# Reordered dilation-4 attention blocks, earlier key staging, and regrouped work in the output projection

## The chip, the cores and the metric

The kernel runs on one core of one Trainium2 chip. The core has five engines with an instruction queue each: TensorE (PE, matmuls; its weight loads are shown as PEld), VectorE (DVE), ScalarE (ACT), GpSimd (POOL) and SyncE (SP), which here does nothing but issue DMAs. The engines run side by side and wait for one another by semaphores. The metric is the device time of one execution in microseconds (us). The kernel before takes 2401.49 us, the median of three runs between 2398.72 and 2403.63. A difference of 0.2% is 4.8 us.

## The reference

One decoder layer over 2048 tokens of width 1024, in float32: a mixer with three head groups (gated linear attention, a gated recurrence, and dilated sliding-window attention), an output projection with a residual, then a gated convolutional FFN. The change touches the dilated attention and the output projection. The attention has six heads of 64 and three patterns:

```python
DILATED_PATTERNS = ((128, 1), (512, 4), (2048, 16))   # (window, dilation)
for window, dil in DILATED_PATTERNS:
    L = S // dil                                      # each residue class mod dil is a sequence of its own
    o, lse = banded_causal_attention(to_sub(q), to_sub(k), to_sub(v), window // dil)
w = softmax(stack(lses), axis=0)                      # the patterns are weighed by their log-sum-exps
o_c = rms_norm(einsum('pbsh,pbshd->bshd', w, stack(outs)), swa_norm)
x = x + concatenate([o_a, o_b, o_c]) @ w_out
```

In banded_causal_attention a block of 128 queries sees its own 128 keys and the 128 before them. The first block of a sequence has no block before it and sees 128 keys only.

## The kernel before

The program runs four parts one after the other: mixer_front, dilated_attention, output_projection and conv_ffn. Between mixer_front and dilated_attention, and between dilated_attention and the output projection, all engines meet at a barrier.

**dilated_attention** goes through 40 turns, one block of queries of all six heads each (attention_blocks, L1180). A turn is j, its block (pattern, residue r, block b). Turns 0 to 15 are dilation 1. Turns 16 to 23 are dilation 16, "double" turns: two residue classes of 128 tokens at once, each with 128 keys. Turns 24 to 39 are dilation 4: before, b is the outer loop, so turns 24 to 27 are the four first blocks (128 keys, `first(j)`), and turns 28 to 39 are full blocks (256 keys).

The engines work on a turn in a pipeline. In iteration j PE does the scores of turn j in three pairs of heads (L1802), and between them it turns the probabilities of turn j-1 (L1814), multiplies them with the values (sums, L1834) and, from turn 24 on, turns the normalised outputs of turn j-3 (L1847). DVE takes the maxima (L1650, L1653, L1658), copies half of the turned probabilities (L1666), finds the lower of two maxima (find_low, L1676), takes the sums (take_sums, L1694), and normalises (L1713, L1717) and stores outputs (take_outputs, L1704). ACT does the exponentials (L1563), the other turned probabilities (L1571) and the weights (L1595). POOL weighs and joins the turn with what an earlier pattern left (L1514, L1519).

The order on each engine is the order of the program text. Points that the change touches:
- **Staging.** For dilation 16 and 4 the keys and queries are gathered with a stride into k_s and q_s, two buffers used by j % 2. POOL copies the keys in `stage(j)` (L1482): two copies for a double turn (L1492), one for a first block (L1494), and three for a full block, its queries included (L1496 to L1498). For double turns and first blocks ACT copies the queries (stage_queries, L1582). PE's scores(j, 0) waits for `staged` and `q_staged`.
- **Weight sums.** Ahead of its first stage POOL does 11 times sum_weights (L1521), four additions on a slab of a later matrix that SP loads and stores again. stage(16) comes after the last of them.
- **Values.** Values in token order lie in v_tok, a ring of 8 slots. SP writes those of dilation 1 to memory (store_values, L1385), and loads them back with a stride (load_values, L1389). Before, a turn of dilation 4 has the slot j % 8. The rows of the earlier pattern are loaded by load_rows (L1401), which waits for `joined` of the turn three before it.
- **Outputs.** The outputs of four turns fill out[:, b % 2]. SP stores them in store_out (L1438) at turns 32 and 36, after load_rows of that SP turn. take_outputs of the first turn of b = 2 (turn 32) waits until store_out(0) has landed, since it overwrites its buffer.

**output_projection** multiplies 32 products n = 8 b + m (b: 512 tokens, m: 128 output columns), each of 8 steps of three matmuls. ACT begins with a table load (L2110). DVE splits the weight slabs (weights_low, L2166), then drains product n into the residual (L2241); PE's product n waits for drain n - 4. After the first product of b = 1, 2, 3 PE sums the squares of block b - 1 (L2262), for which POOL adds them up (L2149) and which ACT turns into a root (L2106).

Of the kernel before, what the change touches and what calls it, by code (L numbers as in the profile page):

```python
# [10 lines left out]
ALU = mybir.AluOpType  # L11
# [5 lines left out]
KT = D // P  # L17
S = 2048
# [1150 lines left out]
SPAN = 128  # L1169
# [13 lines left out]
def attention_blocks():  # L1183


    for b in range(TILES_0):
        yield 0, 0, b
    for r in range(DILATIONS[1]):
        for b in range(2):
            yield 2, r, b  # L1190
    for b in range(S // (DILATIONS[1] * SPAN)):
        for r in range(DILATIONS[1]):
            yield 1, r, b


def dilated_attention(nc, proj_t, ident, swa_gain, v_scratch, o_scratch, mix_t, w_down, s_t,
# [3 lines left out]
    with ExitStack() as ctx:  # L1200
# [112 lines left out]
        def v_slot(j):  # L1313

            return 2 * (j - TILES_0) % V_RING if double(j) else j % V_RING

        def v_half(j, half):

            pat, r, b = blocks[j]
            if pat == 2:  # L1320
                return v_slot(j) + half
            if b == 0:
                return v_slot(j) if half == 0 else (v_slot(j) + V_RING - 1 if pat == 0 else v_slot(j) + 4) % V_RING
            return v_slot(j) if half else (j - (1 if pat == 0 else 4)) % V_RING

        def v_known(engine, j):

            if j < TILES_0:
                engine.wait_ge(v_ready, j + 1)
            elif double(j):  # L1330
                engine.wait_ge(v_in[v_slot(j)], 16 * ((j - TILES_0) // 4 + 1))
            else:
                engine.wait_ge(v_in[v_slot(j)], 16 * ((j - FIRST_1) // V_RING + 1 + (2 if v_slot(j) % 2 == 0 else 0)))
# [39 lines left out]
        def _(sp):  # L1373
# [64 lines left out]
            def store_out(b):  # L1438
                sp.wait_ge(out_ready, 4 * (b + 1))
                sp.dma_start(mix_t[5:8, :, blk(b)].rearrange("g p s -> p g s"), out[:, b % 2, :, :]).then_inc(out_stored[b % 2], 16)  # L1440
# [9 lines left out]
            for j in range(TURNS):  # L1450
# [21 lines left out]
                if j >= FIRST_1 + 8 and (j - FIRST_1) % 4 == 0:  # L1472
                    store_out((j - FIRST_1) // 4 - 2)
# [8 lines left out]
        def _(pool):  # L1482
# [52 lines left out]
            for i in range(KP):  # L1535
                sum_weights(i)
            for j in range(TILES_0 - 1, TURNS + 4):
# [15 lines left out]
        def _(act):  # L1553
# [57 lines left out]
            for j in range(TURNS + 5):  # L1611
# [14 lines left out]
                if TILES_0 <= j + 2 < FIRST_1 + DILATIONS[1]:  # L1626
                    stage_queries(j + 2)
# [11 lines left out]
        def _(dve):  # L1639
# [56 lines left out]
            def take_outputs(i):  # L1696
                f = i - FIRST_1
                b, r = f // 4, f % 4
# [61 lines left out]
        def _(pe):  # L1760
# [10 lines left out]
            def scores(j, g):  # L1771
                pat, r, b = blocks[j]
                if g == 0:
# [5 lines left out]
                    else:  # L1779
                        pe.wait_ge(staged, staged_after(j))  # L1780
                        if double(j) or first(j):
                            pe.wait_ge(q_staged, j - TILES_0 + 1)
# [141 lines left out]
def output_projection(nc, block, used, mix_t, x_t, w_slabs, norm_gain, rstd, x2_t, h_t, origin, w_loaded, mix_loaded, out_stored,  # L1924
# [3 lines left out]
    with ExitStack() as ctx:  # L1928
# [139 lines left out]
        def _(act):  # L2068
# [41 lines left out]
            act.preload_act_table_set("natural_log_exp_and_others")  # L2110
# [46 lines left out]
        def _(dve):  # L2157
# [28 lines left out]
            for n in range(2, OUT_SLABS):  # L2186
                weights_low(n)
# [46 lines left out]

            for b in range(BLOCKS):
                dve.wait_ge(x_loaded[b % 2], 16 * (b // 2 + 1))
                for m in range(KT):
                    n = KT * b + m
                    dve.wait_ge(product_done, n + 1)
                    at = xs[b][:, m, :]  # L2240
                    dve.tensor_tensor(at, banks[n % 4][:, :], at, ALU.add).then_inc(added, 1)  # L2241
# [13 lines left out]
        def _(pe):  # L2255
# [20 lines left out]
            for b in range(BLOCKS):  # L2276
                for m in range(KT):
# [7 lines left out]
                    if n == KT:  # L2285
                        pe.wait_ge(w_ready, 1)
                    cols = slice(m * P, (m + 1) * P)
                    product(pe, banks[n % 4][:, :],
                            [w_hi[:, k, cols] for k in range(KT)], [w_lo[:, k, cols] for k in range(KT)],
                            [mix_hi[b % 2][:, k, :] for k in range(KT)],  # L2290
                            [mix_lo[b % 2][:, k, :] for k in range(KT)], range(KT),
                            mix_ready if b and m == 0 else None, KT * b).then_inc(product_done, 1)
                    if b and m == 0:
                        sum_squares(b - 1)
# [1022 lines left out]
```

## Time and profile before

| | |
|---|---|
| runs | 2398.72, 2401.49, 2403.63 us |
| the profiled execution | 2398.96 us, its span 2397.2 us |
| PE busy, share of the span | 98% |
| DVE, ACT, POOL busy | 72%, 47%, 37% |
| attention turns 16 to 39 | 738.65 to 916.6 us of the span |
| output projection | 919.56 to 1098.9 us |

The busy time of PE counts pipelined matmuls with modelled ends, so it says that PE is hardly ever without work, not that it works at its peak. PEclk is the clock that TensorE was granted, 1.00 for 2.4 GHz and 0.50 for 1.2 GHz. A time in brackets behind a row is how long the engine stood idle before it, and what ended that.

### The profile page before, as it was taken

What the parts mean: (1) busy time and instruction counts of PE and PEld (TensorE: products, weight loads), DVE (VectorE), ACT (ScalarE), POOL (GpSimd) and SP (SyncE); (2) the same over time, 40 slices, a digit from 0 to 9 for tenths busy, and PEclk for the clock granted to TensorE, in tenths of its full rate; (3) what the DMA queues carried; (4) which work ended last, traced back from release to release, by engine and by line L of the source; (5) the groups of instructions that cost most, each with busy time, mean ns of one, the idle gap of its engine ahead of it and who ended that gap; (6) DMA issues with size and microseconds to landing.
All of it is one profiled execution on the core that took longest, in us unless ns stands there. A gap on an engine that the chain in (4) does not pass through costs nothing.

```text
span 2397.2 us, 32989 instructions
## 1 busy us (share of the span) xinstructions
PE 2337.3 (98%) x11664; PEld 1896.7 (79%) x11664; DVE 1719.1 (72%) x2527; ACT 1133.6 (47%) x2026; POOL 888.8 (37%) x705
## 2 busy tenths in 40 slices
PE   8999999999999998999999999999999999999997
PEld 6777888878777776887788888788788888887886
DVE  6454558995455675357888888769979888887655
ACT  6634354332346665225544444545654444445443
POOL 0000003441066672224565656230446565652211
PEclk9999999999999898999999999999999999999999
DMA  5333325553796337374232223598533232337764
GB/s 176 114 98 110 101 83 172 173 178 121 251 313 225 106 105 252 115 254 177 104 125 108 112 102 115 185 307 258 163 125 117 110 110 102 115 117 265 224 197 141
DMA packets 191795, 379.04 MB, mean 158 GB/s; under 512 B 17168, under 2 KB 62864, under 8 KB 182416
## 3 DMA queue, kind: packets, MB, share of 16 engines
q1 hardware_dynamic: 191632, 376.94, 46.3%
q8 instruction: 93, 1.52, 0.3%
q14 instruction: 70, 0.57, 0.1%
HBM read 252.90 MB, written 123.98 MB: 157 GB/s over the span
## 4 chain that ended last, share of the span: by engine, by line
PE 55%; DVE 4%; issue 1%; ACT 1%; DMA 0%; DVEq 0%; ACTq 0%; SPq 0%
PE ff_bank L81 16%; PE ff_bank L82 16%; PE ff_bank L83 16%; PE op_bank L75 2%; PE op_bank L74 2%; PE op_bank L73 2%; DVE ff_ring L3006 1%; DVE ff_b_lo L2948 1%; DVE ff_x_first L3027 0%; DVE ff_y_gate L2993 0%; DVE ff_ring L2954 0%; DVE ff_y_val L2993 0%; PE op_bank L81 0%; DMA ff_raw<-in_slabs 0%; ACT ff_ring L2742 0%
## 5 line engine op out<-in xcount | busy, mean ns | idle before, releaser
L82 PE MATMUL ff_bank<-ff_b_lo,ff_ring 128*128 128x512 f32 x1232 | 479.9, 390 | 0.0
L81 PE MATMUL ff_bank<-ff_b_hi,ff_ring 128*128 128x512 f32 x1056 | 413.2, 391 | 9.5 <-ACT ff_e L2752 5.1
L83 PE MATMUL ff_bank<-ff_b_hi,ff_ring 128*128 128x512 f32 x1056 | 411.7, 390 | 0.0
L73 PE MATMUL ip_bank<-ip_x_hi,ip_w_hi 128*128 128x512 f32 x704 | 289.8, 412 | 12.3 <-DVE ip_x_lo L722 10.6
L74 PE MATMUL ip_bank<-ip_x_lo,ip_w_hi 128*128 128x512 f32 x704 | 276.3, 392 | 0.0
L75 PE MATMUL ip_bank<-ip_x_hi,ip_w_lo 128*128 128x512 f32 x704 | 276.0, 392 | 0.0
L82 PEld LDWEIGHTS ff_bank<-ff_b_lo,ff_ring 128*128 128x128 f32 x1232 | 231.8, 188 | 48.4 <-issue 0.5
L81 PE MATMUL ff_bank<-ff_ring,ff_ring 128*128 128x512 f32 x616 | 241.4, 392 | 2.9 <-DVE ff_ring L3006 2.9
L81 PEld LDWEIGHTS ff_bank<-ff_b_hi,ff_ring 128*128 128x128 f32 x1056 | 198.7, 188 | 54.4 <-issue 7.4
L82 PE MATMUL ff_bank<-ff_ring,ff_ring 128*128 128x512 f32 x616 | 239.7, 389 | 0.0
L83 PE MATMUL ff_bank<-ff_ring,ff_ring 128*128 128x512 f32 x616 | 239.7, 389 | 0.0
L83 PEld LDWEIGHTS ff_bank<-ff_b_hi,ff_ring 128*128 128x128 f32 x1056 | 198.6, 188 | 41.3
L2954 DVE TENSOR_TENSOR ff_ring<-ff_raw,ff_ring 128x512 fp32r<-128x512 f32 x219 | 216.6, 996 | 13.0 <-ACT ff_ring L2742 12.0
L3006 DVE TENSOR_TENSOR ff_ring<-ff_raw_ring,ff_ring 128x512 fp32r<-128x512 f32 x196 | 142.9, 773 | 57.6 <-ACT ff_ring L2790 57.4
L2993 DVE SCALAR_TENSOR_TENSOR ff_y_gate<-ff_u,ff_conv_all,ff_y_gate 128x1024 f32<-128x1024 f32 x88 | 164.1, 1865 | 13.9 <-ACT ff_y_gate L2775 11.3
L73 PEld LDWEIGHTS ip_bank<-ip_x_hi,ip_w_hi 128*128 128x128 f32 x704 | 133.1, 189 | 43.9 <-issue 11.1
L2790 ACT ACTIVATE ff_ring<-ff_raw_ring 128x512 fp32r<-128x512 f32 x196 | 112.3, 623 | 110.6 <-PE ff_bank L83 99.1
L2752 ACT ACTIVATE ff_e<-ff_bank 128x512 f32<-128x512 f32 x132 | 78.5, 595 | 168.3 <-PE ff_bank L83 161.4
L751 DVE TENSOR_TENSOR ip_staged<-ip_bank,ip_rstd 128x512 f32<-128x512 f32 x76 | 52.0, 688 | 144.9 <-PE ip_bank L75 139.3
L75 PEld LDWEIGHTS ip_bank<-ip_x_hi,ip_w_lo 128*128 128x128 f32 x704 | 133.0, 189 | 28.9
L74 PEld LDWEIGHTS ip_bank<-ip_x_lo,ip_w_hi 128*128 128x128 f32 x704 | 133.3, 189 | 27.5 <-issue 2.6
L2993 DVE SCALAR_TENSOR_TENSOR ff_y_val<-ff_u,ff_conv_all,ff_y_val 128x1024 f32<-128x1024 f32 x88 | 114.0, 1296 | 56.6 <-ACT ff_y_val L2775 54.9
(333 smaller groups left out, 4896.4 us busy)
## 6 DMA issues: line engine op xcount, KB each, us to landing
ff_raw<-in_slabs SPq DMA_DIRECT2D x44, 1024.0 KB, 4.9
proj_t<-ip_staged SPq DMA_DIRECT2D x92, 256.0 KB, 2.7
a_t<-ff_y_val SPq DMA_DIRECT2D x44, 512.0 KB, 2.6
t_t<-ff_t_sum SPq DMA_DIRECT2D x88, 256.0 KB, 2.0
ff_raw_ring<-t_t SPq DMA_DIRECT2D x56, 256.0 KB, 4.1
ff_raw_ring<-s_t SPq DMA_DIRECT2D x52, 256.0 KB, 3.3
rp_tables<-in_rope SPq DMA_DIRECT2D x24, 512.0 KB, 4.4
ff_raw_ring<-in_w_down SPq DMA_DIRECT2D x46, 256.0 KB, 3.6
```

The source lines that it names most:

```text
L73: pe.matmul(out, w_hi[k], x_hi[k], start=(k == 0), stop=False)
L74: pe.matmul(out, w_hi[k], x_lo[k], start=False, stop=False)
L75: last = pe.matmul(out, w_lo[k], x_hi[k], start=False, stop=(k == n - 1))
L81: pe.matmul(out, w_hi, x_hi, start=first, stop=False, skip_group_check=resumed)
L82: pe.matmul(out, w_hi, x_lo, start=False, stop=False, skip_group_check=resumed)
L83: return pe.matmul(out, w_lo, x_hi, start=False, stop=last, skip_group_check=resumed)
L751: dve.tensor_tensor(at, bank, scale, ALU.mult).then_inc(bank_free, 1)
L2752: act.activation(e[:, i, :], banks[X[g % 2]][:, :], ACT.Copy).then_inc(e_ready[i], 1)
L2790: act.activation(ring[to][:, 0, :], raw_at(half, n, i), ACT.Copy).then_inc(d_hi_ready, 1)
L2954: dve.tensor_tensor(ring[at][:, 1, :], source(half, m), ring[at][:, 0, :].bitcast(F32), ALU.subtract).then_inc(w_lo_ready, 1)
L2993: dve.scalar_tensor_tensor(out=at, in0=u[:, a, t:t + HALF], scalar=conv_all[:, g, a, t:t + 1], in1=at, op0=ALU.mult, op1=ALU.add).then_inc ...
L3006: dve.tensor_tensor(ring[to][:, 1, :], raw_at(half, n, i), ring[to][:, 0, :].bitcast(F32), ALU.subtract).then_inc(d_lo_ready, 1)
```

## The change

Four things are done.

1. attention_blocks yields the first two blocks of each residue class of dilation 4 together, r0 b0, r0 b1, r1 b0, r1 b1 and so on (turns 24 to 31); turns 32 to 39 stay as they were. The slots of the values follow from r and b, ACT stages the queries of all first blocks, PE's count of `q_staged` is adapted, and store_out(0) and store_out(1) move to SP turns 35 and 36.
2. POOL does stage(16) before the last sum_weights, not after it.
3. The table load at the head of ACT's part of the output projection is gone, and DVE drains products 0 and 1 before it splits the last weight slab.
4. PE's sum of squares stands in the middle of the second product of a block, not behind the first.

```diff
     for r in range(DILATIONS[1]):
         for b in range(2):
             yield 2, r, b
-    for b in range(S // (DILATIONS[1] * SPAN)):
+    for r in range(DILATIONS[1]):
+        for b in range(2):
+            yield 1, r, b
+    for b in range(2, S // (DILATIONS[1] * SPAN)):
         for r in range(DILATIONS[1]):
             yield 1, r, b
...
         def v_slot(j):
 
-            return 2 * (j - TILES_0) % V_RING if double(j) else j % V_RING
+            pat, r, b = blocks[j]
+            return 2 * (j - TILES_0) % V_RING if double(j) else j % V_RING if pat == 0 else r + 4 * (b % 2)
...
-                engine.wait_ge(v_in[v_slot(j)], 16 * ((j - FIRST_1) // V_RING + 1 + (2 if v_slot(j) % 2 == 0 else 0)))
+                engine.wait_ge(v_in[v_slot(j)], 16 * (blocks[j][2] // 2 + 1 + (2 if v_slot(j) % 2 == 0 else 0)))
...
             def store_out(b):
-                sp.wait_ge(out_ready, 4 * (b + 1))
+                sp.wait_ge(out_ready, 7 if b == 0 else 4 * (b + 1))
...
-                if j >= FIRST_1 + 8 and (j - FIRST_1) % 4 == 0:
-                    store_out((j - FIRST_1) // 4 - 2)
+                if j in (FIRST_1 + 11, FIRST_1 + 12):
+                    store_out(j - FIRST_1 - 11)
...
-            for i in range(KP):
+            for i in range(KP - 1):
                 sum_weights(i)
-            for j in range(TILES_0 - 1, TURNS + 4):
+            stage(TILES_0)
+            sum_weights(KP - 1)
+            for j in range(TILES_0, TURNS + 4):
...
-                if TILES_0 <= j + 2 < FIRST_1 + DILATIONS[1]:
+                if j + 2 < TURNS and (double(j + 2) or FIRST_1 <= j + 2 and first(j + 2)):
                     stage_queries(j + 2)
...
-            act.preload_act_table_set("natural_log_exp_and_others")
             for k in range(4):
                 act.sem_inc(mix_hi_ready, 1)
...
-            for n in range(2, OUT_SLABS):
-                weights_low(n)
+            weights_low(2)
...
+            drain(0)
+            drain(1)
+            weights_low(3)
             for b in range(BLOCKS):
...
-                    if b and m == 0:
-                        sum_squares(b - 1)
+                    for ks in (range(KT // 2), range(KT // 2, KT)):
+                        ins = product(pe, banks[n % 4][:, :], ..., ks, ...)
+                        if b and m == 1 and ks[0] == 0:
+                            sum_squares(b - 1)
+                    ins.then_inc(product_done, 1)
```

`drain(n)` is the wait, the addition and the increment that stood in the loop of L2241 before.

## Rows read from the trace of the kernel before

**Rows 1.** The page: busy time of the engines, and the chain that ended last.
```profile
PE 2337.3 (98%) x11664; PEld 1896.7 (79%) x11664; DVE 1719.1 (72%) x2527; ACT 1133.6 (47%) x2026; POOL 888.8 (37%) x705
...
PE 55%; DVE 4%; issue 1%; ACT 1%; DMA 0%; DVEq 0%; ACTq 0%; SPq 0%
```

**Rows 2.** What PE waited for, 690 to 925 us: total, times, longest.
```profile
PE at_s L1791 <- POOL at_k_s L1492: 4.5, 1, 4.5
```

**Rows 3.** Windows cut at PE's scores(j, 0): length, busy by engine, PEclk, DMA.
```profile
738.65:748.12 9.47, 9.47 (x69) 7.59 (x69) 3.57 (x6) 4.07 (x14) 3.07 (x4) 0.74 0.59 200
748.12:755.10 6.98, 6.98 (x68) 5.96 (x67) 4.07 (x8) 5.31 (x16) 0.76 (x3) 1.00 0.56 187
...
802.85:807.00 4.15, 3.91 (x31) 2.91 (x30) 3.43 (x16) 2.41 (x8) 3.93 (x3) 1.00 0.30 108
807.00:811.95 4.95, 4.17 (x32) 3.00 (x31) 3.73 (x18) 3.10 (x10) 3.12 (x6) 0.99 0.53 163
811.95:818.97 7.02, 7.02 (x34) 5.57 (x33) 4.10 (x18) 5.37 (x20) 6.04 (x10) 0.50 0.38 115
818.97:827.28 8.31, 8.31 (x34) 5.58 (x34) 5.24 (x19) 4.35 (x12) 4.22 (x7) 0.50 0.17 49
827.28:836.28 9.00, 9.00 (x52) 6.73 (x52) 5.61 (x19) 4.22 (x11) 4.24 (x7) 0.72 0.16 47
836.28:843.00 6.72, 6.72 (x52) 5.24 (x51) 5.35 (x19) 4.70 (x14) 5.01 (x7) 1.00 0.21 60
```

**Rows 4.** The same columns: a long wait of PE in the FFN.
```profile
1115.00:1130.00 15.00, 10.66 (x39) 8.06 (x38) 14.49 (x16) 7.27 (x14) 7.22 (x5) 0.89 0.15 51
```

**Rows 5.** POOL's timeline: start, length, instruction, idle before.
```profile
731.78 1.27 POOL L1526 TENSOR_TENSOR at_w_sums<-at_w_sums 128x512 f32<-128x512 f32 x1 [2.37 <-DMA at_w_sums<-in_w_down]
...
737.02 3.10 POOL L1492 COPY at_k_s<-at_qkv 128x384 f32<-128x384 f32 x4
```

**Rows 6.** SP's DMA issues, and the DVE instruction that waits for the rows.
```profile
742.01 0.37 SPq L1399 DMA_DIRECT2D at_v_tok<-v_scratch  x1
...
748.72 0.32 SPq L1383 DMA_DIRECT2D o_scratch<-at_o_sb  x1
750.71 0.37 SPq L1412 DMA_DIRECT2D at_rows<-o_scratch  x1
...
754.09 0.17 DVE L1676 TENSOR_TENSOR at_o_sb<-at_neg,at_rows 128x12 f32<-128x12 f32 x1 [0.33 <-DMA at_rows<-o_scratch]
```

**Rows 7.** DMA landing, us: value loads of turns 16, 17; output stores.
```profile
at_v_tok<-v_scratch SPq DMA_DIRECT2D x1, 390.0 KB, 3.6
...
at_v_tok<-v_scratch SPq DMA_DIRECT2D x1, 390.0 KB, 4.2
...
DMA to landing us min/median/max: 3.6/4.5/6.6
```

**Rows 8.** Staging of turn 25, sums of turn 23; copies by form.
```profile
800.38 0.87 POOL L1494 COPY at_k_s<-at_qkv 128x384 f32<-128x384 f32 x1
...
802.95 0.97 DVE L1694 TENSOR_TENSOR at_o_sb<-at_o,at_weight 128x780 f32<-128x780 f32 x1 [1.16 <-PE at_o L1834]
...
L1497 POOL COPY at_k_s<-at_qkv 128x384 f32<-128x384 f32 x12 | 13.9, 1162 | 0.0
...
L1666 DVE COPY at_probs_t<-at_t 128x256 f32<-128x256 f32 x8 | 3.4, 420 | 0.9 <-PE at_t L1814 0.8
```

**Rows 9.** Iteration 36: SP's load of rows, DVE's take_outputs(32), PE's turn_outputs(33).
```profile
878.97 0.32 SPq L1412 DMA_DIRECT2D at_rows<-o_scratch  x1
...
881.03 0.84 DVE L1704 TENSOR_TENSOR at_out<-at_o,at_gain 128x384 f32<-128x384 f32 x1
...
882.02 0.52 PE L1847 MATMUL at_o<-gl_idf,at_o_f 128*128 128x128 f32 x3
```

**Rows 10.** Output projection: ACT's table load, DVE's drain of product 0.
```profile
919.22 1.28 ACT L2110 ACT_TABLE_LOAD   x1 [3.59 <-PEq L64]
...
942.31 0.69 DVE L2241 TENSOR_TENSOR op_x_first<-op_bank,op_x_first 128x512 f32<-128x512 f32 x1
```

More of the change, by code:

```diff
@@ L1323, in v_half @@
                 return v_slot(j) if half == 0 else (v_slot(j) + V_RING - 1 if pat == 0 else v_slot(j) + 4) % V_RING
-            return v_slot(j) if half else (j - (1 if pat == 0 else 4)) % V_RING
+            return v_slot(j) if half else (j - 1) % V_RING if pat == 0 else r + 4 * ((b - 1) % 2)
         def v_known(engine, j):
@@ L1697, in take_outputs @@
                 f = i - FIRST_1
-                b, r = f // 4, f % 4
+                _, r, b = blocks[i]
                 dve.wait_ge(turned_out, f + 1)
@@ L1781, in scores @@
                         if double(j) or first(j):
-                            pe.wait_ge(q_staged, j - TILES_0 + 1)
+                            pe.wait_ge(q_staged, j - TILES_0 + 1 if double(j) else DOUBLE + r + 1)
                 if GROUPS * j + g >= GROUPS * FIRST_1 + 2:
@@ L2185, in _, with drain @@
                 low(0, k)
-            for n in range(2, OUT_SLABS):
-                weights_low(n)
+            weights_low(2)
+            def drain(n):
+                b, m = n // KT, n % KT
+                if m == 0:
+                    dve.wait_ge(x_loaded[b % 2], 16 * (b // 2 + 1))
+                dve.wait_ge(product_done, n + 1)
+                at = xs[b][:, m, :]
+                dve.tensor_tensor(at, banks[n % 4][:, :], at, ALU.add).then_inc(added, 1)
             def norm(b, k):
@@ L2233, in lows_at @@
                 return range(m + 1 if m else 0, min(m + 2, KT))
+            drain(0)
+            drain(1)
+            weights_low(3)
             for b in range(BLOCKS):
-                dve.wait_ge(x_loaded[b % 2], 16 * (b // 2 + 1))
                 for m in range(KT):
[L2238 to L2241, printed above, removed]
+                    if KT * b + m >= 2:
+                        drain(KT * b + m)
                     if b + 1 < BLOCKS:
@@ L2287, in _ @@
                     cols = slice(m * P, (m + 1) * P)
[L2288 to L2292, printed above, removed]
-                    if b and m == 0:
-                        sum_squares(b - 1)
+                    for ks in (range(KT // 2), range(KT // 2, KT)):
+                        ins = product(pe, banks[n % 4][:, :],
+                                      [w_hi[:, k, cols] for k in range(KT)], [w_lo[:, k, cols] for k in range(KT)],
+                                      [mix_hi[b % 2][:, k, :] for k in range(KT)],
+                                      [mix_lo[b % 2][:, k, :] for k in range(KT)], ks,
+                                      mix_ready if b and m == 0 else None, KT * b)
+                        if b and m == 1 and ks[0] == 0:
+                            sum_squares(b - 1)
+                    ins.then_inc(product_done, 1)
         return product_done, added, first_low_ready, slab_summed, summed, square_ready
```

## The prediction

> **What bounds the kernel now.** I read the page first: PE is busy 98% of the span and leads the chain that ended last [rows 1]. So time can come only from PE's waits, or from its clock. Next come PE's waits around the attention. The longest that work inside the attention causes is one of 4.5 us for POOL's staged keys [rows 2]. Third come windows cut at scores(j, 0) [rows 3]. They show what a list of waits can't: two stretches in which PE works at 1.2 GHz. The first holds iteration 16 (9.47 us at a mean clock of 0.74, while iteration 17 with the same work takes 6.98). The second goes from 811.3 to about 832 us and holds iterations 27, 28 and most of 29 (clock 0.50, 0.50, 0.72). Before it PE had waited 4.15 - 3.91 = 0.24 and 4.95 - 4.17 = 0.78 us in the turns with 128 keys. The full turns of dilation 4 behind it run at 1.00 and 6.72 us each.
>
> **Step A, the first staging.** POOL ends sum_weights(9) at 729.4 and then stands idle 2.37 us until the slab of the last one lands at 731.78; the staging starts only at 737.02 [rows 5]. A pair of copies costs 3.10 / 2 = 1.55 us, so stage(16) now runs from 729.4 to 731.0, inside that idle time, and the last sum_weights keeps its times. stage(17) ends at 738.6, before PE asks for it at 741. PE goes from turn 15 into scores(16, 0) at 734.1 without a wait and at full clock: iteration 17 would start at 734.1 + 6.98 = 741.1, not at 748.12. That is 7.0 us: 4.5 of the wait and 2.5 of the clock.
>
> What is late next hangs on SP's queue, which doesn't move. store_values(15) stands in it behind the store of the last weight sums, so the values of turn 16 are loaded only at 742.01 [rows 6], and land 3.6 us later, at 745.6 [rows 7]. PE wants them in sums(16, 0), some 2.6 us into iteration 17, at 743.7: a new wait of 1.9 us. Then the rows: store_sums(15) stood at 748.72 and landed 2.0 us later, and load_rows(16) followed at 750.71. Now the store goes out at about 743.4, right behind the value load of turn 17, which goes out 0.9 us after that of turn 16 and lands 4.2 us later, at 747.1 [rows 7]; so I let the store land at 747.6, an estimate. The rows come 3.3 us after their issue, as from 750.71 to 754.0, at 751.0. DVE's find_low(16), at 754.09 before, wants them at 753.8 - 7.0 + 1.9 = 748.7 and waits 2.3 us. Behind it queue take_sums(16), the maxima of turn 18 and the copy for sums(17, 0), which has some 0.5 us to spare. PE loses 1.7 more. A is worth 7.0 - 1.9 - 1.7 = 3.4 us. Bounds: 7.0 if both loads come early enough, 1 if low clock comes back for a few us.
>
> **Step B, the alternation.** PE's work is the same set of blocks. At full clock, without waits, iterations 25 to 29 would cost 3.91, 3.91, 4.26 (with turn_outputs: 0.52 long, 0.35 until the next [rows 9]), 4.91 (full scores: 8.31 - 7.02 = 1.29 more at 1.2 GHz, so 0.65 at 2.4) and 6.72, together 23.7 us. They took 836.28 - 802.85 = 33.4 [rows 3]. So 9.7 us lie there: 1.0 of waits, 8.7 of clock. The clock part goes if it stays up; the waits change.
>
> - Turn 25 is now a full block. stage(25) is three copies, two like the 0.87 at 800.38 and one of 1.16 [rows 8], some 2.8 us in place of 0.87, and ends at 803.2. PE wanted it at 802.85 (0.35 late). log_weights(23) and ACT's weights(23) queue behind it, so take_sums(23) starts at 803.85, not 802.95. Behind the 0.9 of take_sums come the maxima of two heads at 256 keys, 0.7 (an estimate), and the copy, 0.4: ready at 805.85. PE, with two scores and two turns of probabilities before it, 2.0 us, wants it at 805.25 (0.6 late).
> - Iteration 26 has about 0.2 of the same kind.
> - Later pairs: PE has 4.91 + 6.07 = 10.98 us for a pair (full scores with first sums, and the other way round). DVE is busy 5.35 in a full turn [rows 3]. In the half with full scores only its two copies shrink, to 0.42 each [rows 8], which leaves 4.8 against PE's 4.9; in the other half its maxima shrink, which leaves some 4.5 against 6.1. So PE waits some 0.4 a pair (between 0 and 1), three times. POOL, 5.01 in a full turn and 1.9 less in one that stages a first block, needs 8.1 of 11; ACT is busy 4.70 in a full turn.
>
> Sum of the new waits 0.35 + 0.6 + 0.2 + 1.2 = 2.35 (1 to 4). B is worth 9.7 - 2.35 = 7.35 us at full clock.
>
> **Step C, the store of outputs.** store_out(0) moves from SP turn 32 to 35, behind load_rows(37). That load waits for the join of turn 34 and went out at 878.97, in iteration 36. So the store is issued at 879.3 and lands 3.6 to 6.6 us later, median 4.5 [rows 7], at 883.8. take_outputs(32) overwrites that buffer and stood at 881.03 [rows 9]. It now waits 2.8 us and ends at 884.7. PE's turn_outputs(33) needs it and stood at 882.02. PE loses 2.7 us (1.8 to 4.8); DVE's maxima(36, 2) and take_sums(35) queue behind, but reach the next iteration in time. store_out(1) keeps its place. This step costs 2.7 us that the kernel before doesn't have.
>
> **Steps at nothing.** The table load, 1.28 us at 919.22 [rows 10]: PE's first twelve matmuls run 5 us from 919.56 on at the low clock, and what ACT feeds first, the fifth k, needs a conversion on ACT and one on DVE of 0.7 us each behind the load, so it is ready by 922. No load stood at the head of ACT's attention part either, so none is put in its place. The drains: drain 0 ends at 943.0 [rows 10] and PE's product 4 follows without a wait; it now ends earlier. The slab that moves behind it is for products 6 and 7, two products later. The sum of squares comes half a product, 2.7 us, later; two of its roots stand on ACT behind loads that come later still, and the third is followed by a long idle stretch of ACT. If that cover went, each could cost the 1 or 2 us by which it is late; a gain needs a wait of PE there, and PE has none between 925 and 1098.
>
> The Trainium skill, page "ScalarE: Activation LUTs", section "What ACT_TABLE_LOAD costs", gives about 1283 ns for the load and a drain of about 1380 ns more. The trace has the 1283 but no drain: ACT goes on at 920.51. By either figure the sum stays, as it is ACT's time and not PE's.
>
> **The sum.** -3.4 - 7.35 + 2.7 = -8.0 us. On the profiled execution, 2398.96 us (span 2397.2 and 1.8 around it), that is 2391. The median of the runs is 2401.49, 2.5 above that execution; I take the change from the median: **2393 us**.
>
> **Rivals.**
> 1. *The low clock moves into the alternation and lasts.* For it: before 811.3 PE had waited 0.24 and 0.78 us in two turns, and I forecast 0.35, 0.6 and 0.2 within 8. Once low, the clock stayed low through a turn with full scores and first sums (8.31 us at 0.50), although PE didn't wait, and rose only in a turn of full blocks. The alternation has no such iteration before 32. If it falls in 26 or 27 and stays till 32, 27 us of work cost 8.31 / 4.91 = 1.69 times as much, +18.6, in place of 8.7 before, and the short waits cancel. Total -3.4 + 18.6 - 8.7 + 2.7 = +9: 2411. It is slower than before from an excess of 3.4 + 8.7 - 2.7 = 9.4 us on, about 23 us of low clock (8.7 came of 21). Against it: full blocks carry more work per turn, and in the FFN PE idled 4.3 of 15 us and the clock was at 0.89, 3.3 us of low clock, no more [rows 4].
> 2. *It falls there but comes back as it did.* The excess is 4 to 9 us in place of 8.7, the waits about even; total -5 to 0: 2396 to 2401.
> 3. *The clock falls for some 5 us at A or C*, where PE stands still 1.9 and 2.7 us: +2 to +4 on the forecast, 2396.
> 4. *No new waits at A or C*, because the loads and the store land at their fastest or the order leaves them room: another 3 to 5 us off, 2389.
>
> The Trainium skill's page "TensorE: Matmul & The Clock Gate", section "A second HAM failure mode: psum-queue depth-cycling", says that frequent short idles between groups of matmuls are enough to make the clock swing. The fall at 811.3 after waits of under a us a turn agrees. By that rule the new short waits could bring it down as well, which is rivals 1 and 2; by the rows of full blocks alone it would stay up.
>
> **Chances.** Forecast 0.44 (own range 2389 to 2396), rival 1 0.10, rival 2 0.15, rival 3 0.18, rival 4 0.13. A run of this kernel can tell 0.2%, 4.8 us, from no change. Faster: nearly all of the forecast and of rival 4, and 0.07 of rivals 2 and 3: 0.63. Within 0.2%: 0.26. Slower: rival 1 and an edge of 2: 0.11. The range that leaves out rival 1 and the best of 4 is 2386 to 2404.
>
> **What would show it.** After: no idle before scores(16, 0) and clock 1.00 in iteration 16; a wait of about 2 us at sums(16, 0) and an idle of 2 us for DMA before L1676 of turn 16; clock 1.00 in iterations 25 to 31, 5 to 6 us each; in iteration 36 an idle of 2.8 us on DVE before L1704, ended by the store of outputs, and 2.7 on PE. Wrong would be a clock of 0.5 anywhere between 800 and 840, no wait in iteration 36, or any change of the output projection's length of 179 us beyond 1 us.

## The result and the profile after

The changed kernel takes 2405.1 us (median of 20 runs), the kernel before 2398.5 (median of 20 beside them). The ratio is 1.0028, 95% interval 1.0019 to 1.0037: slower by some 6.7 us, where I had forecast 8.0 faster. (My 2393 stood on the median of three runs of the kernel before, 2401.49, which is 3.0 above that of the twenty; so I compare changes.) The profiled execution spans 2407.8 us, 10.6 more than the one before.

The first view is again the windows cut at PE's scores(j, 0): length, busy time by engine, PEclk, DMA. Iterations 15 to 20 of the changed kernel (they answer to the first two of [rows 3]):

```profile
728.88:736.43 7.55, 7.49 (x59) 5.60 (x58) 4.73 (x8) 4.80 (x10) 6.70 (x7) 1.00 0.99 369
736.43:743.61 7.18, 7.18 (x68) 5.99 (x67) 4.62 (x8) 5.14 (x15) 5.64 (x6) 1.00 0.46 183
743.61:751.92 8.31, 7.21 (x67) 5.98 (x66) 3.89 (x7) 5.14 (x14) 0.00 (x0) 1.00 0.55 149
751.92:764.28 12.36, 9.68 (x67) 8.08 (x66) 4.71 (x9) 7.04 (x17) 8.27 (x11) 0.78 0.70 227
764.28:773.46 9.18, 9.18 (x67) 7.70 (x66) 4.19 (x7) 4.07 (x15) 3.34 (x6) 0.73 0.57 179
773.46:780.43 6.97, 6.97 (x67) 5.96 (x66) 4.32 (x7) 5.44 (x16) 5.25 (x7) 1.00 0.22 55
```

The reader is to see that iterations 15 and 16 are clean, and that iterations 17 to 19 then give it back: a wait of 1.1 us in 17, one of 2.7 in 18, and a low clock behind it. The six iterations take 51.55 us. Before they took 776.01 - 726.62 = 49.39.

Iterations 25 to 32, the alternation (the other rows of [rows 3]):

```profile
807.35:812.51 5.16, 4.55 (x30) 2.92 (x30) 3.95 (x16) 3.09 (x8) 4.43 (x5) 1.00 0.23 80
812.51:818.98 6.47, 5.92 (x50) 4.92 (x49) 4.76 (x18) 3.56 (x12) 5.36 (x9) 1.00 0.57 186
818.98:823.94 4.96, 4.75 (x35) 3.19 (x34) 4.22 (x18) 4.86 (x14) 3.04 (x5) 1.00 0.27 81
823.94:830.67 6.73, 6.38 (x53) 5.27 (x52) 5.08 (x19) 4.77 (x16) 5.20 (x8) 1.00 0.21 63
830.67:835.99 5.32, 4.87 (x35) 3.28 (x34) 4.79 (x19) 4.35 (x12) 2.72 (x5) 1.00 0.26 76
835.99:842.86 6.87, 6.38 (x53) 5.27 (x52) 5.05 (x19) 4.99 (x17) 5.32 (x9) 1.00 0.19 59
842.86:848.80 5.94, 4.86 (x34) 3.27 (x33) 5.42 (x19) 3.67 (x11) 4.68 (x7) 1.00 0.23 72
848.80:855.93 7.13, 6.98 (x52) 5.27 (x52) 5.33 (x19) 5.16 (x15) 5.14 (x8) 1.00 0.19 58
```

The clock stays at 1.00. Length less busy time gives a short wait in every iteration. The eight take 48.58 us, 53.60 before: 5.0 gained.

Iterations 36 to 38, around the store of outputs:

```profile
876.08:885.52 9.44, 6.86 (x53) 5.31 (x52) 5.41 (x19) 4.82 (x15) 5.02 (x7) 0.98 0.37 127
885.52:897.66 12.14, 12.14 (x52) 9.41 (x51) 5.69 (x19) 6.64 (x19) 5.49 (x8) 0.50 0.29 98
897.66:906.48 8.82, 8.82 (x53) 6.54 (x52) 5.61 (x19) 3.10 (x7) 3.80 (x6) 0.74 0.59 173
```

They take 30.40 us, 20.16 before: 10.2 lost, of which 2.6 is a wait. Iteration 37 has no wait at all and takes 12.14 us, because PE runs at 1.2 GHz from end to end. The timelines of SP, DVE and PE show what the wait hangs on (start, length, instruction, idle time before it and what ended it; they answer to [rows 9]):

```profile
878.46 0.32 SPq L1416 DMA_DIRECT2D at_rows<-o_scratch  x1
878.83 0.43 SPq L1444 DMA_DIRECT2D mix_t<-at_out  x1
...
883.14 0.83 DVE L1710 TENSOR_TENSOR at_out<-at_o,at_gain 128x384 f32<-128x384 f32 x1 [2.54 <-DMA mix_t<-at_out]
...
884.12 0.52 PE L1853 MATMUL at_o<-gl_idf,at_o_f 128*128 128x128 f32 x3 [2.58 <-DVE at_out L1710]
```

The same for turn 16 (they answer to [rows 6]): the values of turn 16 go out at 743.66, the store of turn 15's sums at 746.05, and only when that has landed do the rows go out, at 750.88. For PE's wait of 1.10 us at the values the profile names no releaser ("issue"); that it is the load of the values is my reading of the order, and loads_and_store_early below bears it out: with that load earlier the wait is gone.

```profile
743.66 0.37 SPq L1403 DMA_DIRECT2D at_v_tok<-v_scratch  x1
...
746.05 0.42 SPq L1387 DMA_DIRECT2D o_scratch<-at_o_sb  x1
...
747.46 1.08 PE L1840 MATMUL at_o<-at_v_tok,at_probs_t 128*128 128x65 f32 x8 [1.10 <-issue]
...
750.88 0.37 SPq L1416 DMA_DIRECT2D at_rows<-o_scratch  x1
...
754.15 0.17 DVE L1682 TENSOR_TENSOR at_o_sb<-at_neg,at_rows 128x12 f32<-128x12 f32 x1 [3.56 <-DMA at_rows<-o_scratch]
...
757.35 1.11 PE L1840 MATMUL at_o<-at_v_tok,at_probs_t 128*128 128x65 f32 x8 [2.68 <-DVE at_probs_t L1672]
```

The rest of the 10.6 us: turn 15 starts 2.3 us later, the part behind the output projection is 1.6 longer, and the unchanged iterations, the attention's tail and the projection together 0.6 shorter. The projection takes 1108.36 - 928.91 = 179.45 us up to PE's first matmul of the FFN, where it took 1099.36 - 919.56 = 179.80. Nothing that was changed runs in the first of these or the second; over all fourteen profiles below the start of turn 15 lies anywhere between 722.91 and 730.52 us.

### The profile page after: what moved, and what is told of

Same layout as the page of the kernel before. It is cut to its first block, busy times and chain, and to the rows that moved or that the text cites. A ratio compares the mean times of both kernels' runs of the same rounds, so it can differ in the third digit from the quotient of the medians.

```text
span 2407.8 us, 32989 instructions
## 1 busy us (share of the span) xinstructions
PE 2342.9 (97%) x11664; PEld 1900.0 (79%) x11664; DVE 1717.9 (71%) x2527; ACT 1133.4 (47%) x2025; POOL 886.8 (37%) x705
## 4 chain that ended last, share of the span: by engine, by line
PE 55%; DVE 4%; issue 1%; ACT 1%; DMA 0%; DVEq 0%; ACTq 0%; SPq 0%
PE ff_bank L81 16%; PE ff_bank L82 16%; PE ff_bank L83 16%; PE op_bank L74 2%; PE op_bank L75 2%; PE op_bank L73 2%; DVE ff_ring L3021 1%; DVE ff_b_lo L2963 1%; DVE ff_x_first L3042 0%; DVE ff_ring L2969 0%; DVE ff_y_val L3008 0%; DMA ff_raw<-in_slabs 0%; DVE ff_y_gate L3008 0%; PE op_bank L81 0%; DVE ff_x_second L3036 0%
```

## The experiments

Each ran 12 times beside the kernel before, the three repeats of a profile once. All profiles are cut at the same three stretches, and the table after the last experiment has them side by side.

### The store of outputs: store_early and late_store_alone

```diff
-                if j in (FIRST_1 + 11, FIRST_1 + 12):
-                    store_out(j - FIRST_1 - 11)
+                if j in (FIRST_1 + 10, FIRST_1 + 12):
+                    store_out((j - FIRST_1 - 10) // 2)
```

> The changed kernel with store_out(0) one turn of SP's queue earlier: behind load_rows(36) instead of load_rows(37). Nothing else is changed. Theory (step C, with a low clock behind the wait): the store lands near 877, take_outputs(32) finds it done, PE's wait of 2.6 us in iteration 36 goes, and with it the low clock of iterations 37 and 38: iterations 36 to 38 take 20.2 us in place of 30.4, all at clock 1.00, and the time is 10 us under the changed kernel's, about 2395. Rival 1 (the low clock in iterations 37 and 38 has another cause, the short waits of the alternation before it): only the wait goes, 2.6 us, iterations 37 and 38 stay at 12 and 8.8 us, 2402.5. Rival 2 (the store only moves the wait to another turn, since take_outputs waits for other stores too): no gain, 2405.

Measured: 2395.3 us, ratio 0.9989 (0.9975 to 1.0003), 9.8 us under the changed kernel. Iterations 36 to 38 take 6.72, 6.72 and 6.71 us at clock 1.00. One line, one turn of the queue, gives back more than the whole loss of 6.7 us. The theory holds and both rivals fall. Against the kernel before, the 2.9 us that are left can't be told from nothing.

late_store_alone is the reverse, on the kernel before:

```diff
-                if j >= FIRST_1 + 8 and (j - FIRST_1) % 4 == 0:
-                    store_out((j - FIRST_1) // 4 - 2)
+                if j in (FIRST_1 + 11, FIRST_1 + 12):
+                    store_out(j - FIRST_1 - 11)
```

> The kernel before, in its old order of blocks, with nothing changed but store_out(0) put behind load_rows(37) (SP turn 35). Theory: the same wait of 2.6 us in iteration 36 arises, the clock falls behind it, and iterations 36 to 38 take about 30 us in place of 20.2: 10 us slower than the kernel before, ratio 1.004. Rival 1 (my step C): only the wait, 2.7 us, ratio 1.001. Rival 2 (the low clock needs the alternation's short waits ahead of it): the wait, but clock 1.00 behind it, again 2.7 us.

Measured: 2404.7 us, ratio 1.0026 (1.0014 to 1.0039), 6.5 slower than the kernel before. So the late store needs no alternation ahead of it to cost two to three times what its wait is long. The windows of its iterations 36 and 37:

```profile
877.98:888.42 10.44, 7.86 (x52) 6.31 (x51) 5.42 (x19) 5.76 (x19) 5.83 (x8) 0.83 0.34 116
888.42:896.64 8.22, 8.22 (x52) 5.95 (x51) 5.60 (x19) 3.87 (x9) 3.83 (x7) 0.80 0.41 145
```

The wait is 2.58 us as in the changed kernel, but the low clock behind it is shorter (25.4 us for the three iterations in place of 30.4). I had expected about 30, so the size of what the clock adds was not yet understood.

### The early staging: stage_as_before and staging_alone

```diff
-            for i in range(KP - 1):
+            for i in range(KP):
                 sum_weights(i)
-            stage(TILES_0)
-            sum_weights(KP - 1)
-            for j in range(TILES_0, TURNS + 4):
+            for j in range(TILES_0 - 1, TURNS + 4):
```

> The changed kernel with the first staging put back behind the last sum of weights. Theory (step A is worth nothing once the clock falls in iteration 18): PE waits 4.5 us for POOL again before scores(16, 0), the wait of 1.1 us at sums(16, 0) and the one of 2.7 us behind find_low(16) go, the clock falls in iteration 16 only (0.74), and turn 15 to turn 21 take 49.4 us in place of 51.6: the time is 2 us less than the changed kernel's, 2403. Rival (step A is worth the 3.4 us of my prediction and the changed kernel's low clock there is an accident of one execution): 3.4 us more than the changed kernel, 2408.5.

Measured: 2402.6 us, ratio 1.0025 (1.0012 to 1.0038), 2.5 under the changed kernel. That seems to say that step A is a loss. But the intervals overlap, and its profile has turns 15 to 20 at 49.15 us and iterations 36 to 38 at 25.7, not 30.4: most of the difference lay in a stretch that this edit doesn't touch. So step A had to be priced where no late store stands behind it. staging_alone is the same edit the other way round, on the kernel before:

> The kernel before with the early first staging and nothing else. It prices step A where no late store and no alternation stand behind it. Theory (from the profiles so far: turn 15 to turn 21 took 46.8, 46.8 and 51.6 us with the early staging and no other load order, 49.2 to 51.8 with the late one): 1 to 3 us under the kernel before, ratio 0.9990; so step A is a small gain and the 2.5 us by which stage_as_before was under the changed kernel come from the clock behind the late store, 25.7 us there against 30.4 and 31.2. Rival 1: step A is a loss by itself, +2.5 us, ratio 1.001. Rival 2: my step A, -3.4 us, ratio 0.9986.

Measured: 2399.1 us, ratio 1.0000 (0.9987 to 1.0013). By itself step A is worth nothing that can be measured; the interval is 3.1 us to either side, so my 3.4 is out and a loss of 2.5 isn't settled. Its windows show why, iterations 17 and 18:

```profile
739.48:747.88 8.40, 7.21 (x67) 5.98 (x66) 3.89 (x7) 5.14 (x14) 0.00 (x0) 1.00 0.61 180
747.88:759.84 11.96, 10.48 (x68) 8.67 (x67) 4.72 (x9) 7.09 (x17) 8.33 (x11) 0.71 0.70 230
```

The wait for the values and the one for the rows, 1.20 and 1.48 us, are there, and behind them the clock is low for more than before.

### What the staging needs: loads_and_store_early and weights_store_behind_rows

On the changed kernel with the edit of store_early, SP's queue is put in another order:

```diff
-                if 0 <= j - 5 < KP:
+                if 0 <= j - 5 < KP - 1:
                     store_weights(j - 5)
...
+                if 1 <= j <= TILES_0:
+                    store_sums(j - 1)
                 if j == TILES_0 - 1:
                     load_values(TILES_0)
-                if j == TILES_0:
-                    load_values(j + 1)
-                if 1 <= j <= TILES_0:
-                    store_sums(j - 1)
+                    load_values(TILES_0 + 1)
+                    store_weights(KP - 1)
```

> The changed kernel with the early store of outputs, and in SP's queue store_values(15), store_sums(14), load_values(16) and load_values(17) go ahead of the store of the last weight sums, so that store_sums(15) and the rows of turn 16 go out sooner too. Theory: values of turn 16 land near 742 and the rows near 750.5, so the waits of 1.1 us at sums(16, 0) and 2.7 us in iteration 18 shrink to under 1 us in all, the clock stays at 1.00 through iterations 16 to 19, and turn 15 to turn 21 take about 43 us in place of 51.6; with the 10 us of the store: 18 us under the changed kernel, 2387, ratio 0.995 to the kernel before. Rival 1 (the low clock in iterations 18 and 19 does not come from these waits): 4 us of waits go, 2391. Rival 2 (the store's early landing is worth 2.6 us only): 2394 to 2398.

Measured: 2395.2 us, the same as store_early. The expectation of 2387 is missed by 8 us: the wait for the values is gone, but the rows are late as before. Its timelines:

```profile
740.36 0.46 SPq L1429 DMA_DIRECT2D s_t<-at_w_sums  x1
743.90 0.33 SPq L1387 DMA_DIRECT2D o_scratch<-at_o_sb  x1
748.85 0.91 SPq L1416 DMA_DIRECT2D at_rows<-o_scratch  x2
...
752.33 0.17 DVE L1682 TENSOR_TENSOR at_o_sb<-at_neg,at_rows 128x12 f32<-128x12 f32 x1 [3.40 <-DMA at_rows<-o_scratch]
```

and, from the view of its DMA issues between 738 and 752 us (operation, count, KB each, median us from issue to landing):

```profile
s_t<-at_w_sums SPq DMA_DIRECT2D x1, 1024.0 KB, 8.1
o_scratch<-at_o_sb SPq DMA_DIRECT2D x1, 198.0 KB, 4.9
```

The store of sums goes out 2.2 us sooner than in the changed kernel and still takes 4.9 us to land (4.7 there), against 1.9 in the kernel before, where it goes out at a quiet time. What it has beside it is the 1 MB store of weight sums. So the next kernel moves only that one:

```diff
                     load_values(TILES_0 + 1)
-                    store_weights(KP - 1)
                 if j == TILES_0:
                     load_rows(j)
                     load_rows(j + 1)
+                    store_weights(KP - 1)
```

> As loads_and_store_early, but the 1 MB store of the last weight sums goes out behind load_rows(16) and load_rows(17) instead of ahead of store_sums(15). In loads_and_store_early it was issued at 740.36, took 8.1 us to land, and the store of sums issued at 743.90 took 4.9 us beside it where the kernel before has 1.9 at a quiet time; find_low(16) then waited 3.40 us for the rows. Theory: the store of sums lands 2 to 2.5 us after its issue, the rows near 750, find_low(16) waits under 1 us, PE's wait of 2.50 us in iteration 18 goes with the low clock behind it: turn 15 to turn 21 take 43.5 us in place of 49.8, and the time is 6 us under loads_and_store_early, 2389. Rival 1 (the landing is slow for another reason, the value loads beside it): no change, 2395. Rival 2 (the wait goes but the clock falls in any case at this change from turns of 128 keys' staging to doubled blocks): 2.5 us, 2392.5.

Measured: **2389.8 us**, ratio 0.9969 (0.9958 to 0.9980), 9.0 us under the kernel before (4.8 to 10.1 by the ratio) and 15.4 under the changed one. The theory's price was right (6 us under loads_and_store_early expected, 5.5 measured), and its timelines show each step:

```profile
738.94 0.33 SPq L1387 DMA_DIRECT2D o_scratch<-at_o_sb  x1
741.61 0.89 SPq L1416 DMA_DIRECT2D at_rows<-o_scratch  x2
742.55 0.46 SPq L1429 DMA_DIRECT2D s_t<-at_w_sums  x1
...
744.88 0.17 DVE L1682 TENSOR_TENSOR at_o_sb<-at_neg,at_rows 128x12 f32<-128x12 f32 x1 [0.91 <-DMA at_rows<-o_scratch]
```

and the view of its DMA issues has the landing of that store:

```profile
o_scratch<-at_o_sb SPq DMA_DIRECT2D x1, 198.0 KB, 2.6
```

Turns 15 to 20 take 42.4 us with the clock at 1.00 throughout. DVE still waits 0.91 us, and PE none of it.

The Trainium skill, page "DMA: Bandwidth & Descriptors", section "Queues, rings and completion order", says that on each DMA engine the descriptors of one queue are consumed in the order of the ring. The landing of 4.9 us, with the large store issued 3.5 us ahead, is what that order leads one to expect, but two transfers that only share the engines' time could give it too, and no run tells these apart. The 2.6 us say nothing on the order, as the large store went out only at 742.55, when the small one had landed.

### The other two parts: alternation_alone and projection_alone

Both are made on the kernel before. alternation_alone has the new order of blocks, the value slots, counts and staged queries that go with it, and the store at turn 34:

```diff
-    for b in range(S // (DILATIONS[1] * SPAN)):
+    for r in range(DILATIONS[1]):
+        for b in range(2):
+            yield 1, r, b
+    for b in range(2, S // (DILATIONS[1] * SPAN)):
...
-                if j >= FIRST_1 + 8 and (j - FIRST_1) % 4 == 0:
-                    store_out((j - FIRST_1) // 4 - 2)
+                if j in (FIRST_1 + 10, FIRST_1 + 12):
+                    store_out((j - FIRST_1 - 10) // 2)
```

projection_alone has the change's three edits of the output projection and none of the attention:

```diff
-            act.preload_act_table_set("natural_log_exp_and_others")
...
-            for n in range(2, OUT_SLABS):
-                weights_low(n)
+            weights_low(2)
...
+            drain(0)
+            drain(1)
+            weights_low(3)
...
-                    if b and m == 0:
-                        sum_squares(b - 1)
+                        if b and m == 1 and ks[0] == 0:
+                            sum_squares(b - 1)
```

> The kernel before with the alternation of dilation 4's blocks and nothing else: the store of outputs at SP turn 34, the first staging and the output projection as before. Theory (step B alone, as the changed kernel's windows show it: 48.6 us in place of 53.6 for iterations 25 to 32): 5 us under the kernel before, 2393, clock 1.00 in iterations 25 to 31, ratio 0.998. Rival 1 (step B of my prediction, shorter waits): -7.35 us, 2391, ratio 0.997. Rival 2 (the gain of the alternation is partly that of the early staging ahead of it, as the clock is in another state): within 2 us of the kernel before.

Measured: 2395.2 us, ratio 0.9991 (0.9979 to 1.0002): 3.6 under the kernel before by the medians, 2.2 by the ratio, whose interval goes from 5 under to 0.5 over. The time alone doesn't show a gain. The clock is 1.00 in iterations 25 to 31, and the eight take 48.59 us. Rival 1, my own 7.35, is out.

> The kernel before with the changed output projection only: no table load ahead of it, the drains of products 0 and 1 ahead of the third slab's low half, the sum of squares in the middle of the second product. Theory: nothing, ratio 1.000, output projection 179.5 to 179.8 us. Rival: the changed kernel's 0.3 us less there is real and more is lost elsewhere, as the sum of squares comes later: up to 2 us either way.

Measured: 2396.3 us, ratio 0.9995 (0.9982 to 1.0008), no measurable difference. Its profile is worth more than its time: iterations 25 to 28 are those of the kernel before, instruction by instruction, and the last two read

```profile
814.05:820.77 6.72, 6.72 (x34) 5.36 (x33) 4.33 (x18) 5.08 (x19) 5.74 (x10) 0.53 0.32 107
820.77:827.47 6.70, 6.49 (x34) 4.18 (x33) 4.99 (x19) 3.53 (x9) 4.05 (x7) 0.71 0.20 61
```

where [rows 3] has 7.02 at 0.50, 8.31 at 0.50 and a third iteration at 0.72 behind them. The eight iterations take 49.79 us in place of 53.60: in this execution the eight iterations that step B was to shorten were 3.8 us cheaper already.

The fourteen profiles together show a wait in the projection that neither the prediction nor the profile of the kernel before has. In three of the five that keep the old projection PE stands at the sum of squares, behind the first product of a block, for POOL's total: 0.6 us in alternation_alone, 1.4 in staging_alone and 2.0 in staging_and_queue_alone. None of the nine with the new projection has that wait. The projection takes 179.6 to 182.1 us in the five, 180.7 on average, and 179.3 to 180.3 in the nine, 179.7 on average. That is about 1 us, too little for the times to show.

### Does the clock's answer belong to the kernel? changed_third, stage_as_before_again, changed_again

> The changed kernel, unchanged, profiled a second time. Theory: the wait of 2.6 us in iteration 36 is there again to within 0.1 us, since it hangs on the order of the queue, but what the clock does behind it is not fixed: anything from 3 us of low clock (as in stage_as_before and late_store_alone, iterations 36 to 38 in 25.4 to 25.7 us) to 7.5 (30.4 us, the first profile). Rival: the clock follows this kernel's order of work, and iterations 36 to 38 take 30.4 us again; then stage_as_before differs because it is another kernel.

> The changed kernel, profiled a third time. Theory (the clock's answer hangs on which kernel it is and repeats): iterations 36 to 38 in 30.4 to 31.2 us, with clock 0.50 in iteration 37; in iteration 18 a wait of 2.7 us again, with or without low clock behind it, as it was with 10 us of it once and without once. Rival (it is drawn anew in each execution): iterations 36 to 38 in about 25.5 us this time, or a number between.

> stage_as_before profiled a second time: the changed kernel with the first staging behind the last sum of weights. Theory (repeats by kernel): iterations 36 to 38 in 25.7 us. Rival (drawn anew in each execution): 30 to 31 us, as in the changed kernel; then neither kernel's profile says what this wait costs on average, and only the medians do.

Measured: 2404.8, 2404.2 and 2406.1 us in one execution each, and iterations 36 to 38 in 31.24, 26.73 and 32.32 us. The second profile alone spoke for an answer that repeats by kernel, and I bet on that in the two expectations behind it; the third profile and the repeat of stage_as_before (25.7 the first time, 32.3 now) refute it. Even the wait, which I had expected within 0.1 us, came out at 2.58, 3.43 and 3.42. It follows the landing of the store: that took 4.2, 5.1 and 5.1 us in these three profiles, and 4.1, 5.4 and 4.2 where PE waited 2.48, 3.75 and 2.58 (the two of stage_as_before and late_store_alone). What the clock adds does not follow the wait. Iteration 37 of changed_third:

```profile
884.78:893.65 8.87, 8.87 (x53) 6.60 (x52) 5.60 (x19) 3.99 (x10) 3.97 (x7) 0.73 0.39 134
```

The code, the order and the wait of changed_again, and 3.3 us less than its 12.16.

### The old order with the clean start: staging_and_queue_alone

On the kernel before, the two edits already shown, without the alternation and with its stores of outputs untouched:

```diff
+            stage(TILES_0)
+            sum_weights(KP - 1)
...
+                    load_values(TILES_0 + 1)
...
                     load_rows(j + 1)
+                    store_weights(KP - 1)
```

> The kernel before with the early first staging and with the order of SP's queue of weights_store_behind_rows (values of turns 16 and 17, the sums of turn 15 and the rows ahead of the 1 MB store), in the old order of blocks. Theory: turn 15 to turn 21 in 42.4 us without any low clock, as in weights_store_behind_rows, in place of 49.4 to 51.8: 7 to 9 us under the kernel before, 2391, ratio 0.9967. Rival: the clean start of dilation 16 is worth its waits only (5 us), and the 9 us of weights_store_behind_rows are half the alternation's: 2394, ratio 0.998.

Measured: 2392.5 us, ratio 0.9970 (0.9959 to 0.9982), 6.5 under the kernel before (4.3 to 9.8 by the ratio). Turns 15 to 20 take 42.2 us. Iterations 25 to 32 stand in the old order, and in this execution the clock didn't fall in them at all: 47.82 us, less than the alternation's 48.58. Its ratio and that of weights_store_behind_rows can't be told apart, so on top of a clean start the alternation has no measured worth; each interval is over 5 us wide, so a small one isn't ruled out. The new order of the queue was not run with the late staging, so how the gain is shared out between the two edits is open.

Each number below is a difference of starts of scores(j, 0), in us; "PE waits" are the one of POOL's staging or those for the values and rows, and that for the store of outputs. The 2.55 of store_early is for the values and the 2.50 of loads_and_store_early for the rows.

```
profile                     15-20  PE waits     25-32  36-38  PE wait
before                      49.39  4.50         53.60  20.16  -
changed                     51.55  1.10, 2.68   48.58  30.40  2.58
changed_again               46.83  0.77, 2.67   49.70  31.24  3.43
changed_third               52.19  1.22, 2.25   48.58  26.73  3.42
store_early                 46.85  2.55         48.58  20.15  -
stage_as_before             49.15  4.48         48.57  25.72  2.48
stage_as_before_again       50.86  7.10         48.59  32.32  3.75
late_store_alone            51.80  6.92         53.80  25.38  2.58
staging_alone               49.97  1.20, 1.48   53.59  20.16  -
alternation_alone           50.95  6.07         48.59  20.17  -
projection_alone            50.74  5.66         49.79  20.17  -
loads_and_store_early       49.81  2.50         48.55  20.14  -
weights_store_behind_rows   42.38  none         49.74  20.15  -
staging_and_queue_alone     42.23  none         47.82  20.15  -
```

## Why the prediction was wrong, step by step

**What bounds the kernel** held: PE's waits and PE's clock are all that moved. Every wait that I named was found. What failed was the price of the clock: put at nothing behind the new waits of A and C, and counted in full, from one execution, where B was to remove it.

**Step C, "PE loses 2.7 us", is the term that turned the sign.** The mechanism was right to within half a microsecond: store issued at 878.83 (I said 879.3), DVE idle 2.54 (2.8), PE idle 2.58 (2.7). But I closed the sum there, with bounds of 1.8 to 4.8. The step that failed is that sum: it held PE's wait alone and no low clock behind it. The runs put 9.8 us on it in the changed kernel and 6.5 in the kernel before. In the six profiles with the wait, iterations 36 to 38 take 25.4 to 32.3 us, 28.6 on average, so 8.5 over 20.15; of these 3.0 are the wait (2.48 to 3.75) and 5.4 (2.7 to 8.4) PE working at the low clock.

**Step A, "worth 3.4 us", is worth about nothing** (staging_alone: 0.0, 3.1 either way). I took out 2.5 us of low clock with the one wait and put none back behind the two new ones. The waits were as forecast in kind, but shared out otherwise: 1.1 us for the values (I said 1.9) and 2.68 for the rows (1.7), where I let the store of sums land in 4.2 us and it took 4.7. The clock fell behind them in five of the six profiles that have these waits. And the wait that the step removes isn't 4.5 us in every execution: the six profiles with the late staging have 4.5, 4.5, 5.7, 6.1, 6.9 and 7.1.

**Step B, "worth 7.35 us", gave 5.0 in the profiled pair and 3.6 in the medians.** The interval of the ratio includes no change at all. That the clock stays up in the alternation was right. Three sizes were off. The short waits come to 3.9 us, not 2.35, among them PE's of up to 1.1 us for DVE's take_outputs, which I hadn't listed. The low clock that it removed came to 7.9 us in this pair, not 8.7 (PE's busy time in iterations 25 to 32 went from 52.6 to 44.7): iterations 26 to 29 are some tenths dearer at full clock than I had them, 4.14, 4.55, 5.02 and 6.97 in staging_and_queue_alone against 3.91, 4.26, 4.91 and 6.72. And even that isn't the kernel's own: in the five profiles of the old order iterations 25 to 32 took 53.60, 53.80, 53.59, 49.79 and 47.82 us. I read one execution, and it was one of the dear ones.

**The steps at nothing** were nothing that the times show: 179.45 us of output projection against 179.80, and a ratio of 0.9995. But "PE has none between 925 and 1098" was true of one execution only. In three of five profiles of the old projection PE waits 0.6 to 2.0 us at the sum of squares, and in nine of the new one it never does; the profiles put about 1 us on it. The later place of the sum is the likely reason, but no run has it by itself.

**The sum.** By the means of the profiles: A -1.0 (five with the early staging and the old queue 49.5, six with the late one 50.5), B -2.9 (nine profiles of the alternation 48.8, five of the old order 51.7), C +8.5, together +4.6 us; and the medians of the runs give +6.7, 4.6 to 8.9. Hardly any of the error is in the waits: by these means they come out at -2.6 us at A (I said -0.9), +2.3 at B (+1.35) and +3.0 at C (+2.7), in sum 0.4 better than forecast. The low clock is +1.6 at A (-2.5), -5.2 at B (-8.7) and +5.4 at C (0), in sum 13.0 worse. The other 2.1 of the 14.7 us between forecast and medians are not in these means, and means of five to nine profiles that differ by up to 7 us can't settle that much.

**The rivals.** What happened is in the main rival 3, the clock falling at A or C, which I named and gave 0.18; the rest is B's gain, which came out smaller. I priced rival 3 at 2 to 4 us and named no row for it; the only one I gave for low clock behind a long wait is of the FFN, where PE idled 4.3 us and the low clock cost 1.65 [rows 4]. The rows of this very stretch said otherwise: iteration 16, behind a 4.5 us wait, has 2.5 us, and iterations 27 to 29, behind waits under a microsecond, 8.7 [rows 3]. Priced by those, 2.5 to 8.7 at A and again at C, the same rival gives 5 to 17 us on the forecast and covers what happened. Rival 1, the clock low all through the alternation, didn't occur in any of nine profiles. In two of them it fell late, in iteration 32 (8.3 us at 0.79 in place of 7.13), behind the wait of 1.1 us in iteration 31, which the others have too.

The Trainium skill, page "TensorE: Matmul & The Clock Gate", section "A second HAM failure mode: psum-queue depth-cycling", was weighed in the prediction against step B, the place with many short idles. The runs of the alternation hardly bear that out: the clock is 1.00 through its short waits in all nine profiles, up to the fall in iteration 32 in two. In the old order the rule agrees in four profiles of five, where the clock is low from iteration 27 on behind waits under 1 us (in one of them from the end of iteration 26); in the fifth, with waits of the same kind, it isn't low. Apart from all these, the falls came behind single idles of 1.5 to 7.1 us. The same page says, in "What's actually happening", that how much of a kernel's start runs at the low clock differs from run to run. The profiles here agree with that in the middle of a kernel too: 26.7 and 31.2 us behind a wait of 3.42 and 3.43.

## What to carry to other kernels

In a stretch of small matmuls, price a stall of PE of some microseconds by the stall plus the low clock behind it, taken from rows of the same stretch (here 5.4 us on average behind 3.0, and between 2.7 and 8.4), and count it for waits that an edit adds as well as for the one it removes. When a wait is taken away and the time stays, look for the transfer that is late next and for the large one beside it: here the early staging alone changed the time by 0.0 us, and together with a queue in which a 1 MB store no longer stood ahead of a 198 KB one it took 6.5 us off. And take a low clock seen in one profile as one draw: profile a kernel more than once before an edit is credited with removing it.

## What the runs showed of the hardware that was not expected

- The clock's answer to a wait isn't fixed. Behind a wait of 2.7 us in iteration 18 the changed kernel had mean clocks of 0.78 and 0.73 in two iterations once (12.36 and 9.18 us), and in changed_again the clock was not low at all behind it:

```profile
749.14:759.05 9.91, 7.24 (x68) 5.99 (x67) 4.40 (x8) 5.69 (x17) 6.40 (x10) 1.00 0.64 208
759.05:766.02 6.97, 6.97 (x67) 5.95 (x66) 4.32 (x7) 5.44 (x16) 5.25 (x7) 1.00 0.73 228
```

- A clock once low stayed low through 12.14 us of work without a single wait (iteration 37 of the changed kernel), work that takes 6.72 us at 2.4 GHz. Why it rises sooner in some executions is open. No run varied the wait's length by itself, and its length doesn't order the cases: 30.4 us behind 2.58, 26.7 behind 3.42.
- A store of 198 KB took 4.9 us to land beside one of 1 MB issued 3.5 us before it, 2.6 us with that one issued only after it had landed, and 1.9 in the kernel before, at a quiet time.
- A store of 768 KB, the same instruction at the same place, took between 4.1 and 5.4 us to land over six profiles, and PE's wait followed it (2.48 to 3.75 us).
